# A four-layer hybrid decoder step: an output projection in which four tiles follow their inputs, and constant products ahead of first tiles

## What is computed

```python
for l in range(DEPTH):
    nw = p['norm_w'][l]
    h = rmsnorm(x, nw[0])
    kind = LAYER_MIXER[l]            # l % 3: RWKV-7, MLA, gated DeltaNet, RWKV-7
    ...
    x = x + rmsnorm(out.astype(x.dtype), nw[1])
    f, fb = conv_ffn(rmsnorm(x, nw[2]), ffn_conv[l], p, l)
    x = x + rmsnorm(f, nw[3])
```

```python
y = ((y - mu) * lax.rsqrt(var + RW_LNX_EPS)).reshape(B, T, D) * p['rw_lnx_w'][ri] + p['rw_lnx_b'][ri]
...
y = (y + bonus.reshape(B, T, D)).astype(x.dtype) * g
return y @ p['rw_wo'][ri], x[:, -1], S, v_first
```

## Time and profile before

| | us |
|---|---|
| median of 3 runs | 2923.93 |
| lowest and highest | 2922.08, 2924.64 |
| the profiled execution, its own time | 2928.19 |
| span of that execution, first to last instruction | 2926.5 |
| PE busy in it | 2773.7 (95%) |
| DVE, ACT, POOL busy | 1484.7, 1070.5, 573.8 |
| mean granted TensorE clock | 0.981 |

### The profile page before, as it was taken

The page is one execution under the profiler, slowest core; times in us unless marked ns, Lnnn a source line. Parts: engine busy times, 40 slices in busy tenths (PEclk is TensorE's granted clock), DMA queues, the critical chain, the costliest instruction groups (busy, mean ns, idle before and its releaser), DMA issues.

```text
span 2926.5 us, 58889 instructions
## 1 busy us (share of the span) xinstructions
PE 2773.7 (95%) x22823; PEld 2203.7 (75%) x22823; DVE 1484.7 (51%) x3089; ACT 1070.5 (37%) x3237; POOL 573.8 (20%) x737
## 2 busy tenths in 40 slices
PE   7999989999999999999999889899998999999998
PEld 4778757898776667898766777768895678857887
DVE  7554447652243417652642455337726864436661
ACT  2234334422432224531655454325412134324431
POOL 0013110063213200044100222110160003200044
PEclk9999999999999999999999999999999999999999
DMA  5420124444332323433433003533442330123442
GB/s 154 154 72 6 40 70 130 130 139 108 92 104 77 88 77 115 130 128 109 137 110 107 6 6 117 166 109 128 132 136 73 122 102 6 28 63 121 130 131 81
DMA packets 356656, 287.83 MB, mean 98 GB/s; under 512 B 74700, under 2 KB 352764, under 8 KB 355996
## 3 DMA queue, kind: packets, MB, share of 16 engines
q1 hardware_dynamic: 337456, 267.03, 29.6%
q10 hardware_dynamic: 14828, 14.93, 1.5%
q0 software_dynamic: 4096, 2.11, 0.4%
HBM read 263.29 MB, written 20.73 MB: 97 GB/s over the span
## 4 chain that ended last, share of the span: by engine, by line
PE 88%; DVE 6%; issue 2%; ACT 2%; POOL 1%; DMA 0%; ACTq 0%; POOLq 0%; DVEq 0%
PE bank L359 85%; PE bank L3134 1%; POOL arena L1628 1%; PE bank L3157 1%; DVE h L1967 0%; DVE post_scaled L472 0%; DVE x L475 0%; PE bank L1580 0%; DVE arena L2805 0%; DVE small L1399 0%; DVE arena L1515 0%; DVE arena L1517 0%; DVE h L454 0%; DVE arena L1512 0%; PE bank L2265 0%
## 5 line engine op out<-in xcount | busy, mean ns | idle before, releaser
L359 PE MATMUL bank<-h,weights 128*128 128x320 f32 (+2 forms) x3152 | 799.3, 412 | 17.8 <-ACT h L441 17.8
L359 PEld LDWEIGHTS bank<-h,weights 128*128 128x128 f32 (+1 forms) x3152 | 574.0, 191 | 231.5 <-issue 34.3
L359 PE MATMUL bank<-arena,weights 128*128 128x320 f32 (+5 forms) x3088 | 670.7, 377 | 15.6 <-DVE arena L1517 7.6
L359 PE MATMUL bank<-arena 128*128 128x160 f32 (+7 forms) x5034 | 641.8, 292 | 11.9 <-DVE arena L2728 5.1
L359 PEld LDWEIGHTS bank<-arena,weights 128*128 128x128 f32 (+2 forms) x3088 | 507.5, 189 | 161.9 <-issue 26.7
L359 PEld LDWEIGHTS bank<-arena 128*128 128x128 f32 (+2 forms) x5034 | 545.5, 172 | 36.4 <-issue 14.3
L1628 POOL TENSOR_TENSOR arena<-arena,consts 128x256 f32<-128x256 f32 x162 | 118.9, 739 | 767.0 <-DVE arena L1955 450.3
L552 POOL TENSOR_TENSOR arena<-weights 128x512 f32<-128x512 f32 (+1 forms) x48 | 59.9, 1247 | 727.6 <-DMA weights<-ffn_w_down 633.3
L359 PE MATMUL bank<-h,arena 64*64 64x64 f32 (+3 forms) x3000 | 177.0, 233 | 11.6 <-POOL arena L1628 9.7
L359 PEld LDWEIGHTS bank<-h,arena 64*64 64x64 f32 (+1 forms) x3000 | 152.6, 143 | 18.9 <-POOL arena L1628 13.3
L472 DVE SCALAR_TENSOR_TENSOR post_scaled<-h,params,rstd 128x320 f32<-128x320 f32 x64 | 41.5, 648 | 197.3 <-ACT rstd L435 197.3
(11 more groups left out here) (371 smaller groups left out, 3736.7 us busy)
## 6 DMA issues: line engine op xcount, KB each, us to landing
weights<-ffn_w_up SPq DMA_DIRECT2D x88, 1024.0 KB, 5.1
weights<-ffn_w_down SPq DMA_DIRECT2D x32, 1024.0 KB, 5.4
weights<-rw_wrkv SPq DMA_DIRECT2D x24, 1024.0 KB, 5.3
weights<-gdn_w_in SPq DMA_DIRECT2D x24, 1024.0 KB, 5.4
arena<-cache_mla_latent SPq DMA_DIRECT2D x108, 128.0 KB, 2.3
weights<-ffn_w_down SPq DMA_DIRECT2D x16, 768.0 KB, 5.0
weights<-rw_wo SPq DMA_DIRECT2D x8, 1024.0 KB, 5.4
weights<-gdn_wo SPq DMA_DIRECT2D x8, 1024.0 KB, 5.7
```

The source lines that it names most:

```text
L359: return pe.matmul(out, lhsT, rhs, start=first, stop=last, skip_group_check=True)
```

## The change

Two edits, both in PE's program alone.

1. In `pe_rwkv` the four tiles 0 to 3 of the output projection are computed by the new `pe_out_as_ready`: it takes four banks and two weight slots, and for each input n does one product for each of the four tiles. The tiles 4 to 7 follow through `pe_out` as before, now with no wait for inputs.
2. `pe_first_tiles` takes one more bank ahead of its four and does three products of constants into it, `ones` (128 x 128) by the first 320 columns of the constants. Nothing reads the result. Since banks are handed out in turn, all later banks move by one at each of the six places.

```diff
         def pe_first_tiles(pe, q, banks_of, lhsT, done):
 
+            unread = bank(pe, ("unread", q))
+            for i in range(3):
+                mm(pe, unread[:, 0:NT], ones, C[:, 0:NT], True, True)
             outs = [bank(pe, *b) for b in banks_of]
             for k in range(MT):
                 pe.wait_ge(*at("h_raw", (q, k)))
...
-        def pe_out(pe, q, keys, k, ready, rhs):
-
-            for c, slot_keys in enumerate(keys):
+        def pe_out_as_ready(pe, q, keys, ready, rhs):
+
+            ws = [W[:, weight(pe, key), :] for key in keys]
+            outs = [bank(pe, ("out", q, m), ("out", (q, m))) for m in range(2 * len(keys))]
+            for n in range(MT):
+                pe.wait_ge(*at(*ready(n)))
+                for m, ps in enumerate(outs):
+                    ins = mm(pe, ps[:, 0:NT], ws[m // 2][:, n * 256 + m % 2 * P:n * 256 + m % 2 * P + P], rhs(n), n == 0, n == MT - 1)
+                    if n == MT - 1:
+                        ins.then_inc(*to("out_done", (q, m)))
+            for c, key in enumerate(keys):
+                weight_used[key] = ("out_done", (q, 2 * c + 1))
+
+        def pe_out(pe, q, keys, k, ready, rhs, c0=0):
+
+            for c, slot_keys in enumerate(keys, c0):
                 two = len(slot_keys) == 1 and k == 8
...
-            pe_out(pe, q + 1, [[("wo", l, c)] for c in range(4)], 8, lambda n: [("y_gated", (l, n))],
-                   lambda n: block(BA)[:, n, :])
+            pe_out_as_ready(pe, q + 1, [("wo", l, c) for c in range(2)], lambda n: ("y_gated", (l, n)), lambda n: block(BA)[:, n, :])
+            pe_out(pe, q + 1, [[("wo", l, c)] for c in range(2, 4)], 8, lambda n: [], lambda n: block(BA)[:, n, :], 2)
             pe_norm(pe, q + 1)
```

## The result

The changed kernel took 2905.64 us (median of 4 runs, 2900.47 to 2909.12) against 2924.28 us of the kernel before beside it: a ratio of 0.9928 with a 95% interval of 0.9916 to 0.9941. (The ratio and its interval are an estimate from the executions; the two medians alone are 18.6 us apart, which is 0.9936.) That is faster, and inside the stated range of 2889.5 to 2908.5 us, but 8.1 us above the stated 2897.5, and it lies nearer to the 2908.1 of the rival in which the constants don't hold the clock. Only the stretches of the trace tell the two apart.

What follows compares the result with a forecast made beforehand. PE was taken as the bound, busy for 95% of the span. The projection's 15.8 us plus the constants' 10.6 us made 26.4 us, taken from the median 2923.93 us to give 2897.5 us; the range was 2889.5 to 2908.5 us.

Steps and rivals of the forecast that it cites:

- the rival in which the constants don't hold the clock: Gaps before the first tiles: clock falls stay or only move, only the projection's gain remains, 2908.1 us; chance 11%.
- The projection: RWKV output projection, layers 0 and 3: dense block of 34.5 us without waits, saving 8.3 and 7.5 us, sum 15.8.
- the run-in at half clock: Start of layer 3's projection: PE already at half clock, costing 0.6 us in the new order.
- The rival in which the slow clock falls on the start: Projection's start, both layers: a full slow stretch hits dense products, 5.4 us less gained, 2902.9 us; chance 18%.
- The split between idle time and clock: Layer 0's projection: of 8.3 us gained, 5.7 us were idle or thin and 2.6 us were half clock.
- The constants: Six gaps before first tiles: three constant products hold the clock at no cost, gaining 10.6 us (bounds 0 to 10.6).
- The rule of the skill: Basis of a rival: four-bank order keeps PE at 1.2 GHz in both projections, 2932 us; chance 2%.
- The banks: Later banks move by one at six places: put at 0, up to 1 us.
- What could take it back: Behind tiles 0 to 3: ACT's work ends about when tile 4 does, weights load ahead; both taken at nothing.
- the runs' median lies 4.3 us below that execution: Whole kernel: the profiled execution's 4.3 us offset from the runs' median was kept, so 26.4 us came off 2923.93.
- more than forecast: Slow stretches elsewhere happen to move out of dense work, 2889 us or less; chance 6%.

Runs made afterwards that it cites:

- the constants alone: Three constant products at each of the six places, with the old projection, against the kernel before: 2920.17 us, ratio 0.9972.
- the banks alone: One extra bank taken at the six places, without the products and with the old projection, against the kernel before: 2930.10 us, ratio 1.0004.

## Why the prediction was right, and where it was off

**The projection.** Right in each step. One block, no wait, 34.46 and 34.45 us for a stated 34.5. Tiles 0 to 3 in four banks ran at full clock. In layer 3 the run-in at half clock that I had charged 0.6 us for didn't occur (8.17 instead of 7.5 us), nor in any other profile with four tiles: all 16 blocks of eight profiles took 34.45 or 34.46 us. With eight tiles it did, in layer 0, behind a wait of 1.23 us: there the block took 37.03 us instead of 34.69. The rival in which the slow clock falls on the start, for which I gave 18%, was thus seen in none of the 16.

**The split between idle time and clock** in layer 0, 5.7 and 2.6 us, was measured apart: 5.8 and 2.5 us against the same profile. The second varies between executions, as said above.

**The constants.** Right: none of the gaps let the clock fall any more, the products cost nothing, and 40 records take 11.0 us everywhere. The local gain was 10.67 us for a stated 10.6, and what follows in MLP 0 and MLP 1 is as long as before (256.98 us), so it passes the gain on. That the products cost nothing holds where PE has nothing else to do there, and not with eight tiles. What the argument lacked was evidence for where a gap becomes harmless; the run with one product gave it.

**The rule of the skill.** The Trainium skill ("TensorE: Matmul & The Clock Gate", section "A second HAM failure mode: psum-queue depth-cycling") tells of a clock that swings when PE goes round the PSUM banks and idles briefly between the groups. It isn't seen here: the block that goes round four banks has clock 1.00 in both layers. But it has no idle time between its groups either, so the rule as the page states it wasn't put to the test.

**The banks.** Right at 0, as far as it can be told: ratio 1.0004 (0.9995 to 1.0012).

**What could take it back.** ACT was hidden behind tiles 4 to 7, as stated. POOL's sums, which end last, the prediction left out of this reckoning; they were hidden too. The kernel with eight tiles shows the price when that cover is gone: 3.57 us of waiting for POOL, and late first tiles behind it.

**Where it was off.** The stated 2897.5 is 8.1 us below the measured 2905.64. The terms were not mis-sized in the trace; the step that failed is the last, "the runs' median lies 4.3 us below that execution; I take the same difference from it". It treated one median of three runs, and one profile, as if they were fixed. Over its five series the kernel before has 58 runs from 2922.1 to 2934.4 us with a median of 2926.8; the three shown runs lay at the low end. That makes 2.9 us of the 8.1. The four first runs of the change lay 1.6 us above the median of its 14. The remaining 3.6 us are the gain itself, 22.8 us between these two medians instead of 26.4. The parts alone gave 17.9 and 8.2 us, together 26.1, with intervals of 3.5 to 4 us either way, so whether these 3.6 us are chance or an interaction stays open. The traces hint at where some of it lies: the table's first row and its row RWKV 3 together took 845.2 to 846.7 us in the profiles of before, of the constants alone and of the banks alone, and 830.2 to 832.2 in the three of the change, 14.4 us less on average where the two blocks gave 16.5.

That the total fell inside the range was in part luck: the range was made wide for other reasons, and its upper end, 2908.5, is only 2.9 us above the result. It was luck too that the second profile of the change took 2901.8 us, just what was stated for the first, which took 2909.1. No rival named the thing that happened in the first profile: low-clock stretches that move into dense work elsewhere. The case "more than forecast" had it with the sign that is good for the change only, and it should have been given both.

## What to carry to other kernels

When PE is the bound and one output tile waits for each of its inputs in turn, take as many tiles along as make the work for one input slightly longer than the time in which inputs come, and no more: here two left waits, four left none, eight uncovered POOL. Idle time of PE of 2.4 to 3 us ahead of dense work was worth filling with products nobody reads, as long as they waited for nothing and ended before the next real input. Judge such a change by local stretches of the trace; the sum over an execution scattered here by 3 us (standard deviation of the 58 runs before and of the 14 with the change alike).

## What the runs showed that I had not expected

**The clock fell behind dense work.** In the kernel before, PE's windows in RWKV of layer 3, where it was busy without a gap, and its timeline there:

```profile
2316.50:2321.00 4.50, 4.50 (x17) 1.00 0.69 227
2321.00:2325.00 4.00, 4.00 (x10) 0.57 0.70 230
```

```profile
2307.71 8.88 PE L359 MATMUL bank<-arena,weights 128*128 128x320 f32 x32
2316.52 4.57 PE L359 MATMUL bank<-small,weights 32*128 32x320 f32 x16
2321.02 19.19 PE L359 MATMUL bank<-arena,weights 128*128 128x320 f32 x64
```

The 16 records just ahead of the fall, 4.57 us, use 32 rows of the array; the 8.88 us ahead of them use all of it. A busy PE didn't keep the clock there. All 14 profiles show a fall at this place, during these 16 records or within a microsecond of their end. Layer 0 has the narrow and the full products in turn, two records of each (51.2 to 62.9 us), and no fall there. Whether the 32 rows are the cause wasn't tried.

**An operation of DVE tripled in length.** MLP 2 and MLP 3 took 258.07 us in the first profile of the change and 256.99 in the second (both without their first tiles). In the first, this stands ahead of a wait of PE for DVE of 1.10 us:

```profile
2101.11 1.65 DVE L894 SCALAR_TENSOR_TENSOR arena<-arena,params 128x336 f32<-128x336 f32 x1
2101.12 1.27 POOL L568 TENSOR_TENSOR arena<-weights 128x512 f32<-128x512 f32 x1 [1.73 <-DMA weights<-ffn_w_down]
```

and in the second, at the same place:

```profile
2097.18 0.57 DVE L894 SCALAR_TENSOR_TENSOR arena<-arena,params 128x336 f32<-128x336 f32 x1
2097.31 1.57 POOL L568 TENSOR_TENSOR arena<-weights 128x512 f32<-128x512 f32 x1 [1.85 <-DMA weights<-ffn_w_down]
```

When POOL's operation, released by a weight transfer, starts 0.01 to 0.02 us behind DVE's, the latter takes 1.65 us instead of 0.57; when POOL starts 0.13 us later, DVE isn't held and POOL's takes 1.57 instead of 1.27 us. It occurs in 17 of the 56 MLPs of the 14 profiles, with and without the change (in three with the banks alone, in none in the profile of before), each time for 1.0 to 1.1 us. In these 17 POOL starts from 0.08 us ahead of DVE's operation to 0.05 us behind it.
